# A hybrid attention trunk on one core: four k-tiles of x turned by the DMA crossbar, memory scores in split form, a new warm-up

## The chip, the cores and the metric

The kernel runs on one NeuronCore of a Trainium2 chip. The metric is the device time of one execution in microseconds, here the median of three runs. A profiled execution of the same program gives the span, the engine times and the waits that are read below.

## What is computed

The reference, cut to what matters (one layer, batch 1, 256 tokens, width 2048, all float32):

```python
h = rmsnorm(x, norm_mix_g)                      # x: 256 x 2048
proj = h @ w_in                                 # w_in: 2048 x 8192
dq, dk, dv, mq, mk, mv, gate = split(proj)      # 8 differential heads, 8 block heads, gate slab
lam = exp(sum(lq1 * lk1)) - exp(sum(lq2 * lk2)) + 0.2
d_out = rmsnorm((softmax(q1 k1) - lam * softmax(q2 k2)) @ v, subln_g) * 0.8   # causal, ALiBi
m_out = softmax(q k) @ v                        # causal, ALiBi; with 256 tokens only the own block
x = x + (concat(d_out, m_out) * silu(gate)) @ w_out
q = rmsnorm(x, norm_mem_g) @ w_q_mem            # 4 heads of 128
km, vm = split(rmsnorm(mem, mem_norm_g) @ w_kv_mem)
x = x + (softmax(q km / sqrt(128)) @ vm) @ w_o_mem
out = rmsnorm(x, final_g)
```

## The kernel before

Everything large goes through TensorE as a product of split numbers. A float32 operand a is written as hi + lo, both in the fast 32-bit format (fp32r), and a product is hi·hi + hi·lo + lo·hi, three matmuls into one PSUM bank. The weights stream in as "halves" of 2 k-tiles x 512 columns (0.5 MB). SP issues their loads into 8 raw slots (`w_raw`), ACT makes `w_hi` with a copy (`split_hi`), DVE makes `w_lo` with a subtraction (`split_lo`), PE does 12 matmuls of 512 columns per half (`half_group`). A slot is loaded again once DVE has split what was in it: `load_pair_half` waits for `lo_made` to reach the half's number less 7.

The 16 halves of a window are one pair of heads: halves 0 to 7 give the pair's queries and keys, 8 to 15 its values and gate. Eight windows (4 of differential heads, 4 of block heads) are followed by the tail: the output projection, the memory keys and queries, the memory attention, the last projection.

The first window is special, since x has to be turned first: the contraction runs over x's 2048 columns, so PE needs x with its columns on the partitions, as 16 k-tiles of 128 x 256. In `transpose_rows` (line 637) PE turns k-tile k in two fp32 transposes against the identity into a PSUM bank; ACT writes `aT_hi` with the norm's gain (`rows_out_hi`, line 885) and DVE `aT_lo` (`rows_out_lo`, line 1214). `first_half_group` then does, for every k-tile, 2 matmuls of hi·hi (line 650), 2 of lo·hi (line 654), 2 of hi·lo (line 658), each behind a wait for the piece that it uses. `ROWS_BEHIND` says behind which k-tile which later ones are turned: after k-tile 10 the last four, 12 to 15.

Elsewhere the kernel turns float32 data with the DMA crossbar: ACT or DVE writes the low and high 16-bit halves of each number apart ("planes"), SP issues a DMA transpose of the planes, and DVE or ACT merges them again (`turn_qk`, `turn_y`, `split_turn`, `merge_turn`). SP issues these transposes from the same instruction stream as the weight loads.

What sets the order around the change is written out by hand: the list of instructions of each engine, in which the steps above have their places. SP's queue in the first window holds x in five parts and halves 0 to 17.

In the tail, `transpose_queries` (line 761) turns the memory queries, ACT and DVE copy them out of PSUM, and `memory_scores` (line 772) multiplies them with the memory keys in plain fp32: 8 instructions of 256 columns, which the trace shows as 16 passes. Before the first window PE multiplies the identity with itself (`keep_busy`, line 624) 3 times, later 2 times. Three norm vectors (`gains`, 33 rows) are loaded by ACT's DMA queue and turned on PE behind k-tile 1 (line 629). Lambda is brought to all partitions by a product with a row of ones (line 731).

Of the kernel before, what the change touches and what calls it, by code (L numbers as in the profile page):

```python
# [22 lines left out]
F32 = mybir.dt.float32  # L23
# [78 lines left out]
WARM_UP = (3, 2)  # L102
# [31 lines left out]
def program(nc, x, mem, norm_mix_g, w_in, lambda_q1, lambda_k1, lambda_q2, lambda_k2,  # L134
            subln_g, w_out, norm_mem_g, mem_norm_g, w_q_mem, w_kv_mem, w_o_mem, final_g, out):
    with ExitStack() as ctx:
# [24 lines left out]
        ones_row = sbuf("ones_row", [1, P])  # L161
# [6 lines left out]
        gains = sbuf("gains", [2 * KO + 1, P])  # L168
# [30 lines left out]
        r_rows = y_sb[:, :, 0:P]  # L199
        junk_row, _ = carve(pool, 0, DM)  # L200
# [6 lines left out]
        qmT_sb, at = carve(pool, at, 4, SEQ)  # L207
# [20 lines left out]
        assert at <= NT * DM  # L228
        block_planes, block_planesT = [], []
# [65 lines left out]
        gains_loaded = sem("gains_loaded")  # L295
        warm_ready = sem("warm_ready")
# [22 lines left out]
        km_turned = [sem("km_turned0"), sem("km_turned1")]  # L319
        x_summed = sem("x_summed")  # L320
# [5 lines left out]
        ones_ready = sem("ones_ready")  # L326
        lam_made = sem("lam_made")
# [43 lines left out]
        qmT_ready = sem("qmT_ready")  # L371
# [39 lines left out]

        def qm_rows(g, hf):

            if g == 1:
                return kT_rows[:, 2 * hf:2 * hf + 2], (qT_hi, qT_lo)[hf], 0
            if g == 0:
                return cT_hi, cT_lo, 2 * hf
            return yT_hi, yT_lo, (g - 2) * GK + 2 * hf

        def merged_rows(b):  # L420

            source, n = TURNS[b]
            return mems[:, :, n * COLS:(n + 1) * COLS] if source == "mem" else block_planes[b % 2]

# [21 lines left out]
        def _(sp):  # L446
# [56 lines left out]
            for n in range(PAIR_HALVES):  # L503
# [4 lines left out]
                else:  # L508
                    load_pair_half(DIFF, 0, 0, n)
                if n == 6:  # L510
# [61 lines left out]
        def _(pool_e):  # L572
            pool_e.memset(ident[:, :], 0.0).then_inc(ident_ready, 1)
            pool_e.memset(warm, 0.0).then_inc(warm_ready, 1)
# [14 lines left out]
            pool_e.memset(ones_row[:, :], 1.0).then_inc(ones_ready, 1)  # L589
# [3 lines left out]
        def _(pe):  # L593
# [26 lines left out]
            def keep_busy(count):  # L620


                with pe.Fori(0, count):
                    pe.matmul(ps[:, 2, 0:P], ident[:, :], ident[:, :], start=True, stop=True)  # L624

            def transpose_gains():

                pe.wait_ge(gains_loaded, 48)
                pe.transpose(ps[:, 2, 0:2 * KO + 1], gains[:, :], ident[0:2 * KO + 1, 0:2 * KO + 1]
                             ).then_inc(gainsT_made, 1)  # L630
# [9 lines left out]
            def first_half_group(n):  # L640
# [3 lines left out]
                for i in range(GK // 2):  # L644
# [19 lines left out]
                    if k == 1:  # L664
# [43 lines left out]
            def pair_window(j, kind, first=False):  # L708

                for n in range(PAIR_HALVES):  # L710
# [12 lines left out]
                    if first:  # L723
                        if n == 10:
# [6 lines left out]
                            pe.matmul(ps[:, 6, SEQ:SEQ + 1], ones_row[:, :], neg_lam_row[0:1, :], start=True, stop=True  # L731
# [4 lines left out]

            pe.wait_ge(ident_ready, 2)
            keep_busy(WARM_UP[0])
# [27 lines left out]
            def memory_scores():  # L766

                pe.wait_ge(qmT_ready, 2)
                pe.wait_ge(kmT_ready, 2)
# [99 lines left out]
        def _(act):  # L869
# [12 lines left out]
            def rows_out_hi(k):  # L882

                act.wait_ge(rows_made, k + 1)
# [180 lines left out]
            for row, vec in ((0, norm_mem_g), (KO, mem_norm_g)):  # L1065
                act.dma_start(gains[row:row + KO, :], vec[0].rearrange("(k p) -> k p", p=P)).then_inc(gains_loaded, 16)
            act.dma_start(gains[2 * KO:2 * KO + 1, :], subln_g).then_inc(gains_loaded, 16)
# [45 lines left out]
            for i in range(2 * len(TAIL)):  # L1113
# [26 lines left out]
                if i == 48:  # L1140
# [4 lines left out]
                                   ).then_inc(qm_ready, 1)  # L1145
                if i == 49:
# [464 lines left out]
```

## Time and profile before

| | before |
|---|---|
| median of 3 runs | 573.35 us (573.34 to 574.11) |
| the profiled execution, its own time | 572.92 us |
| its span, first to last instruction | 571.1 us |
| PE busy | 562.1 us (98%) |
| DVE, ACT, POOL busy | 425.9, 406.6, 2.1 us |
| mean granted clock of TensorE | 0.996 |
| moved by DMA | 123.32 MB, mean 216 GB/s |

The chain of work that ended last is followed backwards from the last instruction; here PE makes 98% of it. A wait that is not on that chain costs nothing. PE's times in the chain run from the start of one instruction to the start of the next; a busy time of one matmul (some 390 ns for 512 columns) contains the pipeline's own length and overlaps with its neighbours.

### The profile page before, as it was taken

How to read it: one execution, taken by the hardware profiler on the slowest of the kernel's cores; microseconds unless marked ns; L12 is line 12 of the kernel's file. 1: busy time of each engine (PE TensorE's matmuls, PEld its weight loads, DVE VectorE, ACT ScalarE, POOL GpSimd, SP SyncE). 2: the span in 40 equal slices, each digit the busy share in tenths (PEclk: the TensorE clock that was granted, in tenths of full speed). 3: DMA queues.
4: the chain of work that ended last, by engine and by line, in shares of the span. 5: the costliest groups of instructions: out<-in, count | busy, mean ns of one | idle time of the engine just before them, and what ended most of it. 6: DMA issues, size and time to landing. Idle time of an engine off the chain costs nothing.

```text
span 571.1 us, 8602 instructions
## 1 busy us (share of the span) xinstructions
PE 562.1 (98%) x2640; PEld 468.0 (82%) x2640; DVE 425.9 (75%) x716; ACT 406.6 (71%) x651; POOL 2.1 (0%) x26
## 2 busy tenths in 40 slices
PE   8999999999999999999999999999999999999994
PEld 7888888888888888888888888888888888888884
DVE  4769769678886877866756768668568886877975
ACT  5786866967868778776784784875598786855543
POOL 1000000000000000000000000000000000000000
PEclk9999999999999999999999999999999999999998
DMA  8997769568676776886875976779799986983803
GB/s 272 353 280 238 210 173 250 169 201 230 190 233 192 200 216 188 234 224 163 250 215 157 264 199 192 220 194 299 246 229 266 260 248 187 260 230 111 244 2 147
DMA packets 151236, 123.32 MB, mean 216 GB/s; under 512 B 66809, under 2 KB 133162, under 8 KB 150698
## 3 DMA queue, kind: packets, MB, share of 16 engines
q1 hardware_dynamic: 151112, 122.98, 76.3%
q8 instruction: 12, 0.20, 0.1%
q14 instruction: 14, 0.11, 0.1%
q10 hardware_dynamic: 98, 0.03, 0.0%
HBM read 105.93 MB, written 2.10 MB: 189 GB/s over the span
## 4 chain that ended last, share of the span: by engine, by line
PE 98%; DVE 1%; ACT 0%; POOL 0%; issue 0%; ACTq 0%; POOLq 0%
PE ps L614 28%; PE ps L615 28%; PE ps L616 28%; PE ps L697 2%; PE ps L650 1%; PE ps L654 1%; PE ps L658 1%; PE ps L679 1%; PE ps L850 1%; PE ps L855 1%; PE ps L851 1%; PE ps L637 1%; PE ps L772 1%; PE ps L624 0%; PE ps L818 0%; PE ps L682 0%
## 5 line engine op out<-in xcount | busy, mean ns | idle before, releaser
L1209 DVE TENSOR_TENSOR w_lo<-w_raw,w_hi 128x1024 fp32r<-128x1024 f32 x183 | 222.5, 1222 | 106.2 <-ACT w_hi L880 104.2
L880 ACT ACTIVATE w_hi<-w_raw 128x1024 fp32r<-128x1024 f32 x183 | 192.6, 1057 | 82.3 <-PE ps L616 81.3
L614 PE MATMUL ps<-w_hi,aT 128*128 128x512 f32 x540 | 211.8, 392 | 0.0
L615 PE MATMUL ps<-w_lo,aT 128*128 128x512 f32 x540 | 210.3, 389 | 0.0
L616 PE MATMUL ps<-w_hi,aT 128*128 128x512 f32 x540 | 210.1, 389 | 0.0
L616 PEld LDWEIGHTS ps<-w_hi,aT 128*128 128x128 f32 x540 | 101.4, 188 | 21.2
L614 PEld LDWEIGHTS ps<-w_hi,aT 128*128 128x128 f32 x540 | 101.4, 188 | 21.0
L615 PEld LDWEIGHTS ps<-w_lo,aT 128*128 128x128 f32 x540 | 101.4, 188 | 20.4
L614 PE MATMUL ps<-w_hi,yT_hi 128*128 128x512 f32 x144 | 56.2, 390 | 0.0
L616 PE MATMUL ps<-w_hi,yT_lo 128*128 128x512 f32 x144 | 56.0, 389 | 0.0
L615 PE MATMUL ps<-w_lo,yT_hi 128*128 128x512 f32 x144 | 56.0, 389 | 0.0
L615 PEld LDWEIGHTS ps<-w_lo,yT_hi 128*128 128x128 f32 x144 | 27.0, 188 | 5.6
L614 PEld LDWEIGHTS ps<-w_hi,yT_hi 128*128 128x128 f32 x144 | 27.0, 188 | 5.6
L616 PEld LDWEIGHTS ps<-w_hi,yT_lo 128*128 128x128 f32 x144 | 27.0, 188 | 5.5
L1266 DVE RECIPROCAL pool<-pool 128x128 f32<-128x128 f32 x32 | 30.5, 953 | 1.1
L985 ACT ACTIVATE mems<-ps 128x1024 uint16<-128x1024 uint16 x16 | 15.5, 1021 | 17.0 <-PE ps L616 16.9
L1006 ACT ACTIVATE pool<-pool,small 128x256 f32<-128x256 f32 (+1 forms) x48 | 21.2, 444 | 6.9 <-DVE small L1301 6.9
L955 ACT ACTIVATE pool<-mems 128x1024 uint16<-128x1024 uint16 x16 | 21.8, 1365 | 1.1 <-DMA mems<-mems 1.1
L1293 DVE SCALAR_TENSOR_TENSOR pool<-ps,small,alibi 128x256 f32<-128x256 f32 (+2 forms) x32 | 15.0, 511 | 5.9 <-PE ps L685 5.9
L946 ACT ACTIVATE probT<-mems 128x768 uint16<-128x768 uint16 x16 | 16.0, 1077 | 0.0
L1020 ACT ACTIVATE mems<-pool 128x768 uint16<-128x768 uint16 x16 | 13.3, 832 | 2.9 <-DVE pool L1318 2.9
L885 ACT ACTIVATE aT<-ps,gainsT 128x256 fp32r<-128x256 f32 x16 | 7.5, 470 | 8.8 <-PE ps L637 8.7
(202 smaller groups left out, 569.1 us busy)
## 6 DMA issues: line engine op xcount, KB each, us to landing
w_raw<-in_w_in SPq DMA_DIRECT2D x251, 256.0 KB, 3.2
w_raw<-in_w_out SPq DMA_DIRECT2D x64, 256.0 KB, 4.0
w_raw<-in_w_kv_mem SPq DMA_DIRECT2D x32, 256.0 KB, 4.5
w_raw<-in_w_q_mem SPq DMA_DIRECT2D x16, 256.0 KB, 3.0
w_raw<-in_w_o_mem SPq DMA_DIRECT2D x16, 256.0 KB, 3.8
mems<-in_mem SPq DMA_DIRECT2D x1, 2048.0 KB, 10.1
xs<-in_x SPq DMA_DIRECT2D x3, 512.0 KB, 6.3
w_raw<-in_w_in SPq DMA_DIRECT2D x10, 128.0 KB, 5.5
```

The costliest lines, as they stand in the source:

```text
L614: pe.matmul(acc, hi[:, k0 + k, tok], w_hi[:, slot, k], start=first and k == 0, stop=False)
L615: pe.matmul(acc, hi[:, k0 + k, tok], w_lo[:, slot, k], start=False, stop=False)
L616: m = pe.matmul(acc, lo[:, k0 + k, tok], w_hi[:, slot, k], start=False, stop=last and k == GK // 2 - 1)
L880: act.activation(w_hi[:, i % SPLITS], raw, ACT.Copy).then_inc(hi_made, 1)
L946: act.activation(probT[:, u].rearrange("p i q -> p (i q)").bitcast(U16) .rearrange("p (c h) -> p h c", h=2), probT_planes[:, u].rearrange( ...
L955: act.activation(qkT_sb[:, :, t * P:(t + 1) * P].bitcast(U16) .rearrange("p i (q h) -> p h i q", h=2), qkT_planes[:, t].rearrange("p (h i ...
L985: act.activation(qk_planes[:, t].rearrange("p (h c) -> p h c", h=2), ps[:, t, :].bitcast(U16).rearrange("p (c h) -> p h c", h=2), ACT.Copy ...
L1006: m = act.activation(prob_sb[:, u, c, cols], prob_sb[:, u, c, cols], ACT.Exp, bias=neg_max[:, u, t, c:c + 1], accum_out=exp_sum[:, c, u, t ...
L1020: act.activation(prob_planes[:, u].rearrange("p (h c) -> p h c", h=2), prob_sb[:, u, 0, :].bitcast(U16).rearrange("p (c h) -> p h c", h=2) ...
L1209: dve.tensor_tensor(lo, w_raw[:, i % RAW], hi.bitcast(F32), ALU.subtract).then_inc(lo_made, 1)
L1266: dve.reciprocal(s, s).then_inc(silu_steps, 1)
L1293: dve.scalar_tensor_tensor(prob_sb[:, u, 0:kind.maps, cols], banks[:, :, cols], r[:, t:t + 1], bias, ALU.mult, ALU.add).then_inc(logits_re ...
```

## The change

1. **Crossbar.** k-tiles 12 to 15 of x are no longer turned by PE. POOL writes the 16-bit planes of token tile 0 and ACT those of token tile 1 (128 x 1024 half-words each, from x's last 512 columns). SP issues two DMA transposes behind the loads of half 13 (`X_TURN_BEHIND = 13`). DVE merges both tiles (two copies of 128 x 1024 half-words) between the splits of halves 7 and 8, and ACT and DVE make hi and lo of the four k-tiles from SBUF.
2. **x and its order.** x's fifth part is loaded ahead of half 5, no longer ahead of half 6.
3. **Memory scores.** Queries and keys are split into hi and lo (keys: one ACT copy and one DVE subtraction of 128 x 1024; queries: two of each of 128 x 512, in place of one copy on each engine), and the scores are 24 matmuls of 256 columns in fp32r.
4. **Norm vectors.** `gains` is a full 128 x 128 tile, cleared by POOL; its three loads move from ACT's DMA queue to SP's, behind half 2; PE turns it behind k-tile 6 instead of 1.
5. **Warm-up and lambda.** PE multiplies a tile of ones, made by DVE, 5 times (then 2 times) instead of the identity 3 times; lambda is a product over 128 rows with that tile.

The core of the diff; behind the tables of constants and `rows_split` its pieces belong, in this order, to SP, POOL, ACT, DVE and PE:

```diff
-X_PART_BEFORE = (0, 1, 2, None, 3, None, 4, None)
+X_PART_BEFORE = (0, 1, 2, None, 3, 4, None, None)
+X_TURN_BEHIND = 13
-ROWS_BEHIND = {0: (2,), 1: (3,), 2: (4, 5), 4: (6, 7), 6: (8, 9, 10, 11), 10: (12, 13, 14, 15)}
+ROWS_BEHIND = {0: (2,), 1: (3,), 2: (4, 5), 4: (6, 7), 6: (8, 9, 10, 11)}
-WARM_UP = (3, 2)
+WARM_UP = (5, 2)
...
+        def rows_split(t):
+            return (xq_planes[:, t].bitcast(U16).rearrange("p (h c) -> p h c", h=2),
+                    xs[:, t, 3 * COLS:4 * COLS].bitcast(U16).rearrange("p (c h) -> p h c", h=2))
...
+                if n == 2:
+                    sp.wait_ge(gains_zeroed, 1)
+                    for row, vec in ((0, norm_mem_g), (KO, mem_norm_g)):
+                        sp.dma_start(gains[row:row + KO, :], vec[0].rearrange("(k p) -> k p", p=P)
+                                     ).then_inc(gains_loaded, 16)
+                    sp.dma_start(gains[2 * KO:2 * KO + 1, :], subln_g).then_inc(gains_loaded, 16)
+                if n == X_TURN_BEHIND:
+                    for t in range(NT):
+                        sp.wait_ge(xq_planes_ready[t], 1)
+                        sp.dma_start_transpose(xq_planesT[:, t].bitcast(U16).rearrange("p (i q) -> p i q", q=P),
+                                               xq_planes[:, t].bitcast(U16)).then_inc(xq_turned[t], 16)
...
+            out, rows = rows_split(0)
+            pool_e.wait_ge(x_loaded[4], 16)
+            pool_e.tensor_copy(out, rows).then_inc(xq_planes_ready[0], 1)
...
             rows_out_hi(11)
+            out, rows = rows_split(1)
+            act.wait_ge(x_loaded[4], 16)
+            act.activation(out, rows, ACT.Copy).then_inc(xq_planes_ready[1], 1)
             split_hi(7, 7, 0)
+            sum_squares(0, 0)
+            split_hi(8, 8, 0)
             rows_out_hi(12)
-            sum_squares(0, 0)
             rows_out_hi(13)
-            split_hi(8, 8, 0)
+            sum_squares(1, 0)
             rows_out_hi(14)
-            sum_squares(1, 0)
             rows_out_hi(15)
...
             split_lo(7, 7)
+            for t in range(NT):
+                dve.wait_ge(xq_turned[t], 16)
+                dve.tensor_copy(xq_planes[:, t].bitcast(U16).rearrange("p (k q h) -> p h k q", q=P, h=2),
+                                xq_planesT[:, t].bitcast(U16).rearrange("p (h k q) -> p h k q", h=2, q=P)
+                                ).then_inc(xq_merged, 1)
+            split_lo(8, 8)
             rows_out_lo(12)
             rows_out_lo(13)
-            split_lo(8, 8)
...
-                        m = pe.matmul(ps[:, (4, 0)[t] + h // 2, (h % 2) * SEQ:(h % 2 + 1) * SEQ],
-                                      qmT_sb[:, h, t * P:(t + 1) * P], kmT_sb[:, h, :], start=True, stop=True)
+                        pe.matmul(acc, qmT_hi[:, h, tok], kmT_hi[:, h], start=True, stop=False)
+                        pe.matmul(acc, qmT_hi[:, h, tok], kmT_lo[:, h], start=False, stop=False)
+                        m = pe.matmul(acc, qmT_lo[h // 2][:, h % 2, tok], kmT_hi[:, h], start=False, stop=True)
```

How the change moves instructions is shown at three places. The first is SP's queue in the first window, of the changed kernel, from the lambda vectors on. L482 is the weight load (two of 0.25 MB per half: halves 7, 8, 9 and so on), L545 the new transpose.

```order
L482 DMA w_raw<-in_w_in 128x2x256 x2
L482 DMA w_raw<-in_w_in 128x2x256 [waits lo_made]
L482 DMA w_raw<-in_w_in 128x2x256
...
L482 DMA w_raw<-in_w_in 128x2x256 [waits lo_made]
L482 DMA w_raw<-in_w_in 128x2x256
L545 DMA_TRANSPOSE mems<-mems 128x8x128 [waits xq_planes_ready_pool]
L545 DMA_TRANSPOSE mems<-mems 128x8x128 [waits xq_planes_ready_act]
L482 DMA w_raw<-in_w_in 128x2x256 [waits lo_made]
L482 DMA w_raw<-in_w_in 128x2x256
```

The two rows above the transposes load half 13, those below half 14. In the kernel before, nothing stood between them.

The second place is DVE from the split of half 5 on. Before (L1209 is `split_lo`, L1214 `rows_out_lo`):

```order
L1209 TENSOR_TENSOR w_lo<-w_raw,w_hi 128x1024 [waits hi_made]
L1214 SCALAR_TENSOR_TENSOR aT<-ps,gainsT,aT 128x256 [waits rows_hi]
L1209 TENSOR_TENSOR w_lo<-w_raw,w_hi 128x1024 [waits hi_made]
L1214 SCALAR_TENSOR_TENSOR aT<-ps,gainsT,aT 128x256 [waits rows_hi]
L1209 TENSOR_TENSOR w_lo<-w_raw,w_hi 128x1024 [waits hi_made]
L1214 SCALAR_TENSOR_TENSOR aT<-ps,gainsT,aT 128x256 [waits rows_hi] x2
L1209 TENSOR_TENSOR w_lo<-w_raw,w_hi 128x1024 [waits hi_made]
```

and the same place of the changed kernel (L1262 is `split_lo`, L1273 and L1270 are `rows_out_lo` from PSUM and from SBUF, L1476 the merge):

```order
L1262 TENSOR_TENSOR w_lo<-w_raw,w_hi 128x1024 [waits hi_made]
L1273 SCALAR_TENSOR_TENSOR aT<-ps,gainsT,aT 128x256 [waits rows_hi]
L1262 TENSOR_TENSOR w_lo<-w_raw,w_hi 128x1024 [waits hi_made]
L1273 SCALAR_TENSOR_TENSOR aT<-ps,gainsT,aT 128x256 [waits rows_hi]
L1262 TENSOR_TENSOR w_lo<-w_raw,w_hi 128x1024 [waits hi_made]
L1476 COPY mems<-mems 128x2x512 [waits xq_turned0]
L1476 COPY mems<-mems 128x2x512 [waits xq_turned1]
L1262 TENSOR_TENSOR w_lo<-w_raw,w_hi 128x1024 [waits hi_made]
L1270 SCALAR_TENSOR_TENSOR aT<-mems,gainsT,aT 128x256 [waits rows_hi] x2
```

Two merges that wait for the transposes have come in, and the split of half 8 (the row below them) now stands ahead of the low parts of k-tiles 12 and 13.

The third place is PE behind k-tile 10 (L658 and L699 end a k-tile). Before:

```order
L658 MATMUL ps<-w_lo,aT 128x512
L637 MATMUL ps<-ident,xs 128x128 [waits rows_lo,x_loaded4]
L637 MATMUL ps<-ident,xs 128x128
...
L637 MATMUL ps<-ident,xs 128x128 [waits rows_lo,x_loaded4]
L637 MATMUL ps<-ident,xs 128x128
L650 MATMUL ps<-w_hi,aT 128x512 [waits hi_made,rows_hi]
```

and in the changed kernel:

```order
L699 MATMUL ps<-w_lo,aT 128x512
L691 MATMUL ps<-w_hi,aT 128x512 [waits hi_made,rows_hi]
L691 MATMUL ps<-w_hi,aT 128x512
L695 MATMUL ps<-w_hi,aT 128x512 [waits rows_lo]
L695 MATMUL ps<-w_hi,aT 128x512
```

The eight transposes are gone, and k-tile 11 follows k-tile 10 directly. The row that waits for k-tile 12 comes six matmuls later.

## Rows read from the trace of the kernel before

**Rows 1.** The page: its first line and part 1, PE.
```profile
span 571.1 us, 8602 instructions
PE 562.1 (98%) x2640; PEld 468.0 (82%) x2640; DVE 425.9 (75%) x716; ACT 406.6 (71%) x651; POOL 2.1 (0%) x26
```

**Rows 2.** Waits of PE over the span: waited for, us in total, times, longest.
```profile
PE ps L624 <- POOL ident L578: 1.7, 1, 1.7
```

**Rows 3.** The chain that ended last, 22 to 28 us: start, us, what.
```profile
24.21 0.87 PE ps L637 x8
...
26.46 0.45 PE ps L650 x2
26.91 0.45 PE ps L654 x2
```

**Rows 4.** Timeline of SP: weight loads, then the first DMA transposes of the kernel.
```profile
15.05 9.56 SPq L456 DMA_DIRECT2D w_raw<-in_w_in  x14
34.59 3.87 SPq L475 DMA_TRANSPOSE mems<-mems  x2
```

**Rows 5.** DMA, 0 to 24.66 us and 0 to 34.59 us: all that was moved.
```profile
DMA packets 7163, 7.56 MB, mean 307 GB/s; under 512 B 538, under 2 KB 6394, under 8 KB 7162
...
DMA packets 10765, 11.04 MB, mean 319 GB/s; under 512 B 751, under 2 KB 9996, under 8 KB 10764
```

**Rows 6.** Line L475, then L482, both 128 x 1024 half-words: from issue to landing.
```profile
L475 SPq DMA_TRANSPOSE mems<-mems x16: 1234/1242/2397, 34.6 to 359.2; - x16
DMA to landing us min/median/max: 3.1/3.3/5.3
...
L482 SPq DMA_TRANSPOSE pool<-mems x7: 1231/1232/1571, 92.1 to 368.2; - x7
DMA to landing us min/median/max: 4.7/5.0/6.2
```

**Rows 7.** SP and DMA at 36 us: the second transpose's issue and its landing.
```profile
36.05 2.40 SPq L475 DMA_TRANSPOSE mems<-mems  x1
...
mems<-mems SPq DMA_TRANSPOSE x1, 4.6
```

**Rows 8.** Timeline of ACT and DVE, 22 to 24 us.
```profile
22.13 0.47 ACT L885 ACTIVATE aT<-ps,gainsT 128x256 fp32r<-128x256 f32 x1
...
22.50 1.22 DVE L1209 TENSOR_TENSOR w_lo<-w_raw,w_hi 128x1024 fp32r<-128x1024 f32 x1
```

**Rows 9.** Groups by form: plane copy, merge, low part from SBUF (mean ns).
```profile
L917 ACT ACTIVATE pool<-xs 128x1024 uint16<-128x1024 uint16 x8 | 8.3, 1043 | 0.0
...
L1229 DVE COPY mems<-pool 128x1024 uint16<-128x1024 uint16 x8 | 5.6, 750 | 0.0
L1240 DVE SCALAR_TENSOR_TENSOR aT<-mems,gainsT,aT 128x256 fp32r<-128x256 f32 x16 | 6.7, 477 | 0.0
```

**Rows 10.** The chain at the start: k-tile 0, and the gains' transpose.
```profile
5.62 1.04 PE ps L650 x2
6.66 0.46 PE ps L654 x2
...
9.66 0.18 PE ps L629
```

**Rows 11.** Busy times by stretch: PE, PEld, DVE, ACT, POOL, granted clock, DMA share, GB/s.
```profile
566.20:571.00 4.80, 0.00 (x0) 0.00 (x0) 0.81 (x3) 1.07 (x2) 0.00 (x0) 0.50 0.61 219
```

**Rows 12.** Tail: the chain at the memory scores; timeline of 256-column matmuls and of PE's last.
```profile
518.44 3.45 PE ps L772 x16
...
562.29 0.28 PE L850 MATMUL ps<-w_hi,cT_hi 128*128 128x256 f32 x1
562.41 0.28 PE L851 MATMUL ps<-w_lo,cT_hi 128*128 128x256 f32 x1
...
563.25 0.64 PE L855 MATMUL ps<-w_hi,cT_lo 128*128 128x256 f32 x4
```

**Rows 13.** Timeline of weight loads into PE at the start.
```profile
7.60 0.20 PEld L637 LDWEIGHTS ps<-ident,xs 128*128 128x128 f32 x2 [0.45 <-DMA xs<-in_x]
```

More of the change, by code:

```diff
@@ L167, in program @@
         mix_gain = sbuf("mix_gain", [KO, P])
-        gains = sbuf("gains", [2 * KO + 1, P])
+        gains = sbuf("gains", [P, P])
         gainsT = sbuf("gainsT", [P, 3 * KO + 1])
@@ L199, in program @@
         r_rows = y_sb[:, :, 0:P]
+        ones = r_row[:, 0:P]
         junk_row, _ = carve(pool, 0, DM)
@@ L410, in program @@
         kT_rows = kT_parts[:, :, :, :].rearrange("p u r s -> p (u r) s")
+        qmT_hi = kT_rows
+        qmT_lo = (qT_hi, qT_lo)
+        kmT_hi, kmT_lo = cT_hi, cT_lo
         def qm_rows(g, hf):
@@ L573, in _ @@
             pool_e.memset(ident[:, :], 0.0).then_inc(ident_ready, 1)
+            pool_e.memset(gains[:, :], 0.0).then_inc(gains_zeroed, 1)
             pool_e.memset(warm, 0.0).then_inc(warm_ready, 1)
@@ L623, in keep_busy @@
                 with pe.Fori(0, count):
-                    pe.matmul(ps[:, 2, 0:P], ident[:, :], ident[:, :], start=True, stop=True)
+                    pe.matmul(ps[:, 2, 0:P], ones, ones, start=True, stop=True)
             def transpose_gains():
                 pe.wait_ge(gains_loaded, 48)
-                pe.transpose(ps[:, 2, 0:2 * KO + 1], gains[:, :], ident[0:2 * KO + 1, 0:2 * KO + 1]
-                             ).then_inc(gainsT_made, 1)
+                pe.transpose(ps[:, 2, 0:P], gains[:, :], ident[:, :]).then_inc(gainsT_made, 1)
             def transpose_rows(k):
@@ L730, in pair_window @@
                             pe.wait_ge(lam_ready, 2)
-                            pe.matmul(ps[:, 6, SEQ:SEQ + 1], ones_row[:, :], neg_lam_row[0:1, :], start=True, stop=True
+                            pe.matmul(ps[:, 6, SEQ:SEQ + 1], ones, neg_lam_row[:, :], start=True, stop=True
                                       ).then_inc(lam_made, 1)
@@ L882, in rows_out_hi @@
             def rows_out_hi(k):
+                if k >= 3 * GK:
+                    act.wait_ge(xq_merged, NT)
+                    rows, hi = rows_turned(k, aT_hi)
+                    act.activation(hi, rows, ACT.Identity, scale=gainsT[:, k:k + 1]).then_inc(rows_hi, 1)
+                    return
                 act.wait_ge(rows_made, k + 1)
@@ L1145, in _ @@
                                    ).then_inc(qm_ready, 1)
+                    act.wait_ge(kmT_ready, 2)
+                    act.activation(kmT_hi[:, :, :], kmT_sb[:, :, :], ACT.Copy).then_inc(kmT_hi_ready, 1)
                 if i == 49:
-                    act.wait_ge(qmT_made, 1)
-                    act.activation(qmT_sb[:, 0:2].rearrange("p h s -> p (h s)"), ps[:, 4, :], ACT.Copy
-                                   ).then_inc(qmT_ready, 1)
+                    for b in range(2):
+                        act.wait_ge(qmT_made, b + 1)
+                        act.activation(qmT_hi[:, 2 * b:2 * b + 2], ps[:, 4 + b, :].rearrange("p (h s) -> p h s", s=SEQ),
+                                       ACT.Copy).then_inc(qmT_hi_ready, 1)
                 if i == 41:
@@ L1401, in row_rms @@
                 rsqrt(r, ms, newton[:, 0:NT], steps, extra + 1)
+            dve.memset(ones, 1.0).then_inc(ones_ready, 1)
+            dve.memset(neg_lam_row, 0.0).then_inc(lam_zeroed, 1)
             dve.wait_ge(gainsT_made, 1)
```

50 lines of the change are left out of this document (37 added, 13 removed).

## The prediction

> **What bounds the kernel now.** I read the page first, then PE's waits, the chain, and last SP and the DMA in the first 35 us. PE is busy for 98% of the span [rows 1], and its only wait for another engine is one of 1.7 us at the start [rows 2]; beside it stands a gap of 0.45 us at 7.60 for the second part of x [rows 13]. So every microsecond that PE is spared comes off the time, and every microsecond that it waits is added: nothing later takes a wait back. SP and the DMA don't appear there, because the weights come early enough. How early, and over what queue, decides this change: from 15.05 to 24.61 SP issues 14 weight loads, halves 7 to 13 [rows 4], and at 24.66 only 7.56 MB have been moved [rows 5].
>
> **What PE is spared.** The eight transposes of k-tiles 12 to 15 take 0.87 us [rows 3]. The gains' transpose goes from behind k-tile 1, 0.18 us [rows 10], to behind k-tile 6, where a transpose of 128 columns costs 0.87/8 = 0.11: 0.07 less. The memory scores take 3.45 us now; the new ones are 24 matmuls of 256 columns, which follow each other at 562.41 - 562.29 = 0.12 us [rows 12], so 2.88 and 0.57 less. Together 1.5 us, if nothing else happened: 573.35 - 1.5 = 571.8.
>
> **Edits that I cost at nothing.** The longer warm-up and its tile of ones come before 7.60, where PE waits 0.45 us for x anyway [rows 13]. An earlier rise of the clock would only lengthen that wait. If the ten passes ran late they have the same 0.45 us; beyond that it is a loss of some tenths. The lambda product keeps its passes. The gains' loads put three more issues into SP's queue, 0.5 us each at most by the weight loads beside them; the queue of data behind SP is then megabytes long, so the DMA has work meanwhile. The extra splits of the scores' operands (one ACT copy of about 1 us [rows 9], one DVE subtraction of 1.22 us [rows 8], and four short ones) stand beside matmuls of the half in between, 12 times 0.23 us [rows 10]; they cost something only if the queries' low parts come later than 2.7 us after their transpose, and then DVE is what PE waits for.
>
> **The crossbar path, step by step.** PE now needs k-tile 12 at 26.46 - 0.87 - 0.07 = 25.5 [rows 3]. When does it get it?
>
> 1. *Planes.* ACT copies token tile 1 after `rows_out_hi(11)`, which ends at 22.60 [rows 8]; the copy takes 1.04 us [rows 9], so 23.65. POOL has no such copy in this trace. It starts once x's last part is there, and has until the queue below is empty; it costs nothing up to several microseconds, and I take nothing.
> 2. *Issue.* SP reaches the transposes behind half 13's loads, at about 24.6 [rows 4].
> 3. *The queue.* All these transfers are of SP's queue. By 24.6 it holds x (2.10 MB) and 14 halves (14 x 0.524 = 7.34 MB), 9.44 MB, of which 7.56 are moved [rows 5]. The other 1.88 MB are ahead of the transposes. From 24.66 to 34.59 the DMA moves 11.04 - 7.56 = 3.48 MB, 0.35 MB per us, so they need 5.4 us: until 30.0. That transposes do wait behind loads shows in two lines with the same shape: those of L475, issued mostly with little ahead, land 3.3 us after issue, those of L482, issued among weight loads, 5.0 [rows 6].
> 4. *Landing of both.* The nearest case is the pair at 34.59 [rows 4]. By then 2.10 + 18 x 0.524 = 11.53 MB had been issued and 11.04 moved; the last 0.49 MB went by 36.0. The second landed 4.6 us after 36.05, at 40.65 [rows 7]: 4.65 us behind an empty queue. The other end: its issue long done, the pair needs the 3.3 us of a lone one [rows 6]. Behind 30.0 this gives 33.3 to 34.65. I take 34.0, in the middle, since SP can issue the first of the two early but is itself held back by the full queue.
> 5. *Merge.* The second merge takes 0.75 us [rows 9]: 34.75. ACT's high part (0.47 us) lets PE start the first pair of k-tile 12 at about 35.2.
> 6. *Low part.* DVE first splits half 8, 1.22 us [rows 8], then makes the low part of k-tile 12, 0.48 us [rows 9]; overlapped as they usually are 1.65 us together: 36.4. Only then can the third matmul of k-tile 12 run. In the kernel before it ran at 26.91 [rows 3].
>
> So that matmul is 36.4 - 26.9 = 9.5 us later than before, the savings ahead of it included. Behind it DVE is ahead of PE again (low parts of 0.48 us against 1.38 us of matmuls per k-tile), and the buffers are full.
>
> **The clock.** PE stands still from 25.5 to 35.2. At the end of the kernel the clock stands at 1.2 GHz (0.50) from 566.20 on [rows 11], less than 3 us after PE's last matmuls began at 563.25 [rows 12]; so it falls in this gap. At the start PE worked from 1.7 on [rows 2] and the rate doubled around 6.4: two matmuls of 512 columns took 1.04 us at 5.62 and 0.46 at 6.66 [rows 10]. With the same 4.7 us of slow clock from 35.2 on, the part behind 36.4, 3.5 us, does half its work: 1.75 us lost. The bounds are nothing and some 3 us. The Trainium skill has this too (TensorE: Matmul & The Clock Gate, section "HAM oscillation — how this bites in real kernels"): a wait for DMA brings the slow clock back, in its case with 1.67 us at the slow clock per gap, half of it lost; by that figure the loss would be 0.8 and the time 583.1. This trace shows the longer phase at its start, and I go by it.
>
> **The sum.** +9.5 (stall, with PE's savings before it) + 1.75 (clock) - 0.57 (scores) = +10.7. The profiled execution took 572.92 us, 0.43 less than the median, so 583.6 against itself and **584.0** against the median of 573.35.
>
> A second page bears on step 4 (the Trainium skill, DMA: Bandwidth & Descriptors, section "Latency and other measured facts"): a DMA transpose moves 261 GB/s. An estimate by it: 0.52 MB take 2.0 us behind 30.0, and the sum is 582.0. The pair in this trace took 4.65 us, which decides against it.
>
> **Rivals.**
>
> - *A. The clock stays up, or falls only briefly.* The stall is as above, the 1.75 us are not lost: 582.2. For it: nothing in this trace shows a gap of PE in the middle. Against it: the drop at the end [rows 11].
> - *B. The transposes don't queue behind the loads.* Then the second is issued at 24.6 + 1.24 and lands 3.3 us later [rows 6], at 29.1; merge, split and low part end at 31.5; the third matmul is 4.6 us late, the clock costs 1.75 more: 573.35 + 4.6 + 1.75 - 0.57 = 579.1. Against it: L482's 5.0 us, and that step 3 counts 1.88 MB ahead of them.
> - *C. Not slower: the turned rows are there when PE comes.* Its place is the gap ahead of k-tile 12, its price the 1.5 us of PE work alone: 571.8, faster by 0.27%. It decides if both transposes have landed by about 23.8, for merge, high part and low part to be ready at 25.5 to 26. SP would have to reach them by 20. For it: SP's pace is set by the full queue, which x's earlier fifth part reorders. Against it: the load of half 13 waits for the split of half 5, and ACT's planes exist only at 23.65. Even an empty queue gives B. The break-even is a stall of 1.5 us.
> - *D. Longer.* SP can't issue the transposes before the queue has nearly drained, or the slow clock holds longer than at the start: 34.65 in step 4 and up to 3 us for the clock give 586.
>
> **How the numbers follow.** The forecast gets 0.66, A 0.14, B 0.10, D 0.06, C 0.04. What is told apart from no change is 0.2%, 1.1 us. Slower by more: forecast, A, B and D, 0.96. Faster by more: nearly all of C, 0.03. Within: 0.01. The range takes the forecast with step 4's ends and the clock's bounds (33.3 and no loss give 581.5; 34.65 and 3 us give 586), and goes down to B: **578.5 to 586.5**.
>
> **What would show it.** In the changed kernel's profile: PE's waits gain one, of 9 to 10 us, ahead of k-tile 12, released by ACT's high part, and a shorter one for DVE's low part behind it. DVE waits some 8 us for the transpose ahead of its merges (L1476). The transposes (L545) take 8 us and more to land. The granted clock of the stretch 30 to 40 us is below 1. The chain loses the eight transposes, and the scores (L816 to L818) take 2.9 us. The prediction is wrong if the transposes land within 4 us of their issue (B), if PE's wait is under 2 us (C), if the scores cost more than 3.45 us because PE waits there for DVE, or if a stall of this size stands and the time is nevertheless under 580, which would mean that PE's work is not what sets the end.

## The result, and the profile after

The changed kernel takes **583.72 us** (median of 4 executions, 583.35 to 584.15) against 573.35: a ratio of 1.0178, 95% interval 1.0163 to 1.0192, slower by 10.4 us. The forecast was 584.0, range 578.5 to 586.5. The execution that was profiled took 584.15; its span is 582.3, 11.2 more than in [rows 1], and the mean granted clock of TensorE is 0.984 (before 0.996). Two executions far outside the rest, one of the kernel before (2025.54 us) and one of a later experiment (1468.61 us), are in none of the medians, ratios and intervals below.

First the page of the kernel after, the lines that answer to [rows 1], and the granted clock in tenths over 40 slices of the span:

```profile
span 582.3 us, 8623 instructions
...
PE 564.2 (97%) x2644; PEld 469.6 (81%) x2644; DVE 429.5 (74%) x722; ACT 409.7 (70%) x654; POOL 3.1 (1%) x27
...
PEclk9959999999999999999999999999999999999998
```

PE is busy 2.1 us longer than before, though it has less to do, and the third slice (29 to 44 us) stands at 5 tenths. So the 11.2 us are a stall, and slower work behind it. The wait of PE, then those of ACT and DVE on the same chain (us in total, times, longest):

```profile
PE ps L691 <- ACT aT L932: 9.5, 1, 9.5
...
ACT aT L932 <- DVE mems L1476: 7.5, 1, 7.5
DVE mems L1476 <- DMA mems<-mems: 6.9, 2, 6.7
```

(PE's only other wait is one of 1.1 us at the start, for DVE's tile of ones, where the kernel before waits 1.7 [rows 2].) Read from top to bottom these are one event: PE waits for the high part of k-tile 12, ACT for the merge, DVE for the DMA transpose. The timelines of SP and DVE (start, us, engine and operation, in brackets the idle time before it and what ended it):

```profile
16.34 9.63 SPq L482 DMA_DIRECT2D w_raw<-in_w_in  x14
26.01 5.95 SPq L545 DMA_TRANSPOSE mems<-mems  x2
...
33.05 0.74 DVE L1476 COPY mems<-mems 128x1024 uint16<-128x1024 uint16 x1 [6.69 <-DMA mems<-mems]
33.97 0.74 DVE L1476 COPY mems<-mems 128x1024 uint16<-128x1024 uint16 x1 [0.18 <-DMA mems<-mems]
34.60 1.21 DVE L1262 TENSOR_TENSOR w_lo<-w_raw,w_hi 128x1024 fp32r<-128x1024 f32 x1
```

And the line of the transposes (duration of an issue in ns, least, median and most; first and last start), with its time from issue to landing:

```profile
L545 SPq DMA_TRANSPOSE mems<-mems x2: 2350/2950/3549, 26.0 to 29.6; - x2
...
DMA to landing us min/median/max: 4.3/5.7/7.0
```

SP reaches the pair at 26.01, is held in it for 5.95 us, and the second lands at 33.95, 2.0 us after its issue has ended. The chain that ended last, from there to the first matmul of half 8:

```profile
29.61 4.33 DMA mems<-mems
...
33.97 0.75 DVE mems L1476
34.74 0.52 ACT aT L932
...
35.30 1.22 PE ps L691 x2
36.52 0.95 PE ps L695 x2
37.48 0.85 PE ps L699 x2
...
40.89 0.68 PE ps L691 x2
41.57 0.47 PE ps L695 x2
...
43.88 0.23 PE ps L656
```

L695 at 36.52 is the third matmul of k-tile 12, which ran at 26.91 [rows 3]: **9.61 us** later. The 0.85 us per two matmuls behind it are the slow clock (0.45 to 0.47 once it is over, at 41.57). Half 8 begins at 43.88, in the kernel before at 31.97:

```profile
31.97 0.23 PE ps L614
```

That is 11.91 us later, so in this execution the slow clock cost 11.91 - 9.61 = **2.30 us**. The granted clock by stretch (column behind POOL's busy time; then DMA share and GB/s):

```profile
24.50:27.00 2.50, 1.27 (x5) 0.68 (x4) 1.24 (x2) 2.47 (x4) 0.00 (x0) 1.00 1.11 349
27.00:30.00 3.00, 0.00 (x0) 0.00 (x0) 0.00 (x0) 0.22 (x1) 0.00 (x0) 0.60 1.10 346
...
35.30:41.20 5.90, 5.90 (x14) 4.38 (x15) 3.67 (x8) 3.45 (x7) 0.00 (x0) 0.50 0.57 186
41.20:43.90 2.70, 2.70 (x13) 2.21 (x12) 1.23 (x1) 2.67 (x4) 0.00 (x0) 0.99 0.52 178
```

From here on the two kernels run alike, and the lag shrinks twice. At the lambda product it goes from 11.91 to 11.63 (L772 here, L731 in the kernel before). At the memory scores (chain, 24 matmuls from 530.14 to 533.01, one each 0.12 us) it goes from 11.70 to 11.12, with no wait for DVE or ACT. The kernel before at the lambda product, then the kernel after at both places:

```profile
40.36 0.31 PE ps L731 x2
40.67 0.43 PE ps L614
```

```profile
52.27 0.12 PE ps L772 x2
52.38 0.34 PE ps L656
...
530.14 0.12 PE ps L816
530.25 0.12 PE ps L817
```

The books of the span: +9.61 + 2.30 - 0.28 (lambda product) - 0.58 (scores) = +11.05, and the spans differ by 11.2.

### The profile page after: what moved, and what is told of

Read it like the earlier page. It is cut to its first block, busy times and chain, and to the rows that moved or that the text cites. A ratio compares the mean times of both kernels' runs of the same rounds, so it can differ in the third digit from the quotient of the medians.

```text
span 582.3 us, 8623 instructions
## 1 busy us (share of the span) xinstructions
PE 564.2 (97%) x2644; PEld 469.6 (81%) x2644; DVE 429.5 (74%) x722; ACT 409.7 (70%) x654; POOL 3.1 (1%) x27
## 4 chain that ended last, share of the span: by engine, by line
PE 94%; SPq 2%; DMA 1%; DVE 1%; ACT 1%; issue 0%; ACTq 0%
PE ps L656 27%; PE ps L657 27%; PE ps L658 27%; PE ps L738 2%; SPq L482 1%; PE ps L720 1%; PE ps L895 1%; PE ps L900 1%; PE ps L896 1%; PE ps L691 1%; PE ps L695 1%; PE ps L699 1%; DMA mems<-mems 1%; DMA w_raw<-in_w_in 1%; SPq L545 1%; PE ps L863 0%
## 5 line engine op out<-in xcount | busy, mean ns | idle before, releaser
L1262 DVE TENSOR_TENSOR w_lo<-w_raw,w_hi 128x1024 fp32r<-128x1024 f32 x183 | 222.7, 1222 | 107.8 <-ACT w_hi L925 105.8
L656 PE MATMUL ps<-w_hi,aT 128*128 128x512 f32 x540 | 211.7, 392 | 0.0
L658 PE MATMUL ps<-w_hi,aT 128*128 128x512 f32 x540 | 210.2, 389 | 0.0
L658 PEld LDWEIGHTS ps<-w_hi,aT 128*128 128x128 f32 x540 | 101.4, 188 | 21.2
L656 PEld LDWEIGHTS ps<-w_hi,aT 128*128 128x128 f32 x540 | 101.4, 188 | 21.0
L658 PE MATMUL ps<-w_hi,yT_lo 128*128 128x512 f32 x144 | 56.0, 389 | 0.0
L658 PEld LDWEIGHTS ps<-w_hi,yT_lo 128*128 128x128 f32 x144 | 27.0, 188 | 5.6
L691 PE MATMUL ps<-w_hi,aT 128*128 128x512 f32 x32 | 12.2, 469 | 9.7 <-ACT aT L932 9.5
L691 PEld LDWEIGHTS ps<-w_hi,aT 128*128 128x128 f32 x32 | 6.5, 222 | 11.4 <-ACT aT L932 10.0
```

Of the source, the lines that this page charges most:

```text
L656: pe.matmul(acc, hi[:, k0 + k, tok], w_hi[:, slot, k], start=first and k == 0, stop=False)
L658: m = pe.matmul(acc, lo[:, k0 + k, tok], w_hi[:, slot, k], start=False, stop=last and k == GK // 2 - 1)
L691: pe.matmul(ps[:, t, :], aT_hi[:, k, t * P:(t + 1) * P], w_hi[:, slot, i], start=first, stop=False)
L1262: dve.tensor_tensor(lo, w_raw[:, i % RAW], hi.bitcast(F32), ALU.subtract).then_inc(lo_made, 1)
```

## The experiments

All are edits of the kernel after, unless said otherwise; the ratio is always to the kernel before on the same chip (medians there 573.35 to 573.77).

**Does the place in SP's list set the stall?** The edit is one constant, earlier by two halves, or later (15):

```diff
-X_TURN_BEHIND = 13
+X_TURN_BEHIND = 11
```

> The changed kernel with the transposes two halves earlier in SP's queue (behind half 11, not 13). Theory (the pair waits for all bytes that stand ahead of it): 1.05 MB less ahead, at 0.35 MB per us 3.0 us; the pair lands at 31 in place of 34, PE's wait ahead of k-tile 12 falls from 10.0 to 7 us, the time to 580.7 us. Rival (the pair takes as long as it takes once planes exist, 24.1 us, since the crossbar is slow under load): landing stays near 34, the time 583.7. Second rival (SP's place doesn't matter because ACT's planes come late): under 1 us gained.

> The changed kernel with the transposes two halves later (behind half 15). Theory: 1.05 MB more ahead, 3.0 us later, PE's wait 13 us, 586.7 us. Rival (the pair's landing is set by its planes and the crossbar): 583.7.

Measured: 580.48 us, ratio 1.0120 (1.0099 to 1.0141), and 586.01 us, 1.0220 (1.0199 to 1.0241). PE's wait is 6.5 and 12.3 us. SP's timeline and DVE's second merge, behind half 11:

```profile
23.82 6.03 SPq L545 DMA_TRANSPOSE mems<-mems  x2
...
31.88 0.74 DVE L1476 COPY mems<-mems 128x1024 uint16<-128x1024 uint16 x1 [0.16 <-DMA mems<-mems]
```

and behind half 15:

```profile
28.59 6.04 SPq L545 DMA_TRANSPOSE mems<-mems  x2
...
36.69 0.74 DVE L1476 COPY mems<-mems 128x1024 uint16<-128x1024 uint16 x1 [0.17 <-DMA mems<-mems]
```

The three kernels have one picture, shifted: the pair's issue takes 6.0 us, and the second merge comes 2.0 to 2.1 us behind its end (29.85, 31.96, 34.63 against 31.88, 33.97, 36.69). Each place of two halves is worth 2.1 to 2.7 us of the merge, where the theory had 3.0, and 2.3 to 3.2 of the time (it had 580.7 and 586.7). The landing follows the number of loads ahead.

A rival that the two edits can't tell apart from this is a fixed delay of some 4 us between SP's arrival and the first packet. The packets under 512 B show it in slices of 0.2 us (a transpose's have 0.25 KB): they set in at 28.0, 29.8 and 32.8, that is 4.2, 3.8 and 4.2 us after SP's arrival, with 1.6, 1.5 and 1.6 MB of x and weights issued and not yet moved. The pair of [rows 4] had only 0.49 MB ahead, and its packets set in at 35.8, 1.2 us after 34.59. So the delay goes with the bytes ahead, and a fixed one is ruled out. It is the same 4 us in the three kernels because SP itself runs about 1.6 MB ahead of the DMA in each.

**Does it wait behind SP's queue, or behind the DMA's work?** Here ACT issues the two transposes, in its own queue; they stand in its list behind its plane copy, and each waits only for its planes:

```diff
-                if n == X_TURN_BEHIND:
-                    for t in range(NT):
-                        sp.wait_ge(xq_planes_ready[t], 1)
-                        sp.dma_start_transpose(xq_planesT[:, t].bitcast(U16).rearrange("p (i q) -> p i q", q=P),
-                                               xq_planes[:, t].bitcast(U16)).then_inc(xq_turned[t], 16)
...
+            for t in range(NT):
+                act.wait_ge(xq_planes_ready[t], 1)
+                act.dma_start_transpose(xq_planesT[:, t].bitcast(U16).rearrange("p (i q) -> p i q", q=P),
+                                        xq_planes[:, t].bitcast(U16)).then_inc(xq_turned[t], 16)
```

> The changed kernel with both transposes issued by ACT, right behind its plane copy (24.1 us), so in a DMA queue of their own; SP's queue holds loads only. Theory (waiting behind the loads in the same queue is what makes them late): they land 3.3 to 5 us after issue, at about 28 and 30; merges done by 31; PE's wait is 6 us, the time about 579 to 580. Rival (the DMA engines are full, whatever the queue): the pair lands near 34, 583.7 us; it may even be later, since ACT's split of half 7 moves behind two issues.

Measured: 584.29 us, ratio 1.0196 (1.0176 to 1.0215). Not faster: my theory of "behind the loads of the same queue" fell in this form. Its timelines of ACT's queue and of DVE:

```profile
21.82 1.41 ACTq L1134 DMA_TRANSPOSE mems<-mems  x1
...
24.20 2.95 ACTq L1134 DMA_TRANSPOSE mems<-mems  x1
...
30.84 0.74 DVE L1475 COPY mems<-mems 128x1024 uint16<-128x1024 uint16 x1 [1.27 <-DMA mems<-mems]
34.54 0.74 DVE L1475 COPY mems<-mems 128x1024 uint16<-128x1024 uint16 x1 [2.96 <-DMA mems<-mems]
```

And its DMA queues in 25 to 26, in 25 to 28 and in 28 to 30 us (packets, MB, share of 16 engines; in 25 to 26 there is no row but the one shown):

```profile
q1 hardware_dynamic: 359, 0.35, 110.0%
...
q10 hardware_dynamic: 502, 0.13, 24.5%
...
q1 hardware_dynamic: 569, 0.55, 80.7%
q10 hardware_dynamic: 569, 0.14, 32.3%
```

ACT's first is issued 4.2 us earlier than SP's was (it waits for POOL's planes alone and goes out before ACT's own plane copy has run), yet the second lands at 34.5. q10 is ACT's queue. It moves nothing before 26.0, 4.2 us after its first transpose was issued, though POOL's planes had been ready since 20.2 and nothing else stood in that queue. At 21.82 SP had issued x and the loads up to half 10 (7.86 MB, and one or two loads more), of which 6.38 MB were moved; those 1.5 MB take 4.2 us at 0.35 MB per us. So a queue of its own didn't pass the backlog: the pair waited as long as in SP's queue. Why it waits for loads of the other queue no run shows; that the time fits their bytes is an estimate. Behind 26.0, while both queues have work, the DMA engines take one packet of each in turn (569 and 569): a load's packet has about 1 KB, a transpose's 0.25, so each small packet pays for a large one. The 2112 packets of the two transposes take until 34.5. What the pair waits for is the full DMA, by either queue. The Trainium skill has the sharing (DMA: Bandwidth & Descriptors, section "Issuing engines are not separate DMA queues"): transfers interleave on the same 16 engines whoever issues them. The trace agrees, with its 569 packets of each queue.

**What did the clock cost?** PE fills its gap with products of ones, into a bank that nobody reads, so that it doesn't stand still (`GAP` is 40, then 25):

```diff
+                    if k == 3 * GK:
+                        with pe.Fori(0, GAP):
+                            pe.matmul(ps[:, 3, P:2 * P], ones, ones, start=True, stop=True)
```

> The changed kernel with 40 products of the tile of ones put ahead of k-tile 12, into a PSUM region that nobody reads (some 8.5 us at the fast clock), so that PE waits as long for x but is not idle. Theory (2.3 us of the 10.4 lost are the slow clock behind the wait): granted clock 1.00 from 35 us on, k-tiles 12 to 15 take 1.38 us each again, the time 581.4 us. Rival (those k-tiles are slow for want of operands, not of clock): no change, 583.7. If the loop outlasts the wait, its excess is added.

Measured: 586.87 us, ratio 1.0235 (1.0218 to 1.0252). The loop was longer than the gap: 40 products took 15.07 us, and the third matmul comes at 41.21 in the chain, 4.7 later than in the kernel after. The clock did stay up: two matmuls take 0.46 us from there on. By the sum +4.7 - 2.3 the profiled execution would be 2.4 slower; the spans (584.7 and 582.3) differ by 2.4. With 25 products:

> As gap_busy with 25 products instead of 40. There 40 of them took 14.9 us, 5.4 longer than PE's wait, though the clock stayed at 1.00 behind them and k-tiles 12 to 15 took 1.37 us each. 25 should take 9.3 us, as long as the wait. Theory (the slow clock behind the wait costs 2.3 us): 581.4 us. Rival (the filling itself slows DVE, ACT or the transposes by what it saves): 583.7.

Measured: 582.36 us, ratio 1.0155 (1.0139 to 1.0172); the intervals of this and of the kernel after overlap, the medians differ by 1.4. The trace shows it directly. Its busy times by stretch (columns as above):

```profile
35.00:42.00 7.00, 6.11 (x27) 4.60 (x27) 5.76 (x10) 6.31 (x11) 0.00 (x0) 1.00 0.67 200
```

And its chain from the third matmul of k-tile 12 on, with the last two of half 7:

```profile
36.82 0.73 PE ps L699 x2
37.55 0.46 PE ps L703 x2
...
41.64 0.45 PE ps L703 x2
```

The granted clock is 1.00 at once, and the stretch from the third matmul (L699 here) to half 8 takes 42.10 - 36.82 = 5.28 us, where the kernel after needs 43.88 - 36.52 = 7.36 and the kernel before 5.06. Against the profiled execution of the kernel after, the slow clock is worth 2.1 to 2.3 us. The idle gap is its cause: filling the gap with useless work takes it away.

Its size is another matter. The other kernels with a gap ahead of k-tile 12 have the same matmuls behind it, so the same subtraction can be done in each (starts in the chain; the slow phase runs from PE's first matmul behind the gap to the rise of the granted clock; the loss is the time from the third matmul to half 8, less the 5.06 us of the kernel before):

| kernel | PE's wait | slow phase | third matmul | half 8 | lost |
|---|---|---|---|---|---|
| kernel after | 9.5 | 5.9 | 36.52 | 43.88 | 2.30 |
| pair in ACT's queue | 10.1 | 4.8 | 37.10 | 43.90 | 1.74 |
| pair behind half 15 | 12.3 | 3.9 | 39.24 | 45.60 | 1.30 |
| low parts first (below) | 8.6 | 3.9 | 35.52 | 41.87 | 1.29 |
| pair behind half 11 | 6.5 | 3.7 | 34.44 | 40.74 | 1.24 |
| early pair (below) | 4.2 | 4.7 | 31.53 | 38.40 | 1.81 |

In all six the granted clock is 0.50 behind the gap, and the length of the slow phase doesn't go with the length of the gap. So 2.30 is the largest of six readings, from one execution each, and 1.2 to 1.8 is what the others show. The 1.4 us between the medians of the kernel after and of the kernel with 25 products is nearer to those.

**Is the low part behind half 8's split worth anything?** DVE makes the low parts of k-tiles 12 and 13 first:

```diff
-            split_lo(8, 8)
...
             rows_out_lo(13)
+            split_lo(8, 8)
```

> The changed kernel with DVE making the low parts of k-tiles 12 and 13 ahead of the split of half 8. Theory: k-tile 12's low part is ready 0.9 us earlier, but PE's first pair of that k-tile takes 0.85 us at the slow clock, so its third matmul moves from 36.52 to about 36.15: 0.4 us less, 583.3 us. Rival (the split of half 8 is what comes late then): no change.

Measured: 583.72 us, ratio 1.0170 (1.0156 to 1.0184). In its trace the low part is ready in time, but the first two matmuls behind the gap take 1.22 us anyway (the expectation had 0.85), and the third comes at 35.52 behind a start at 34.30: the same 1.22 as from 35.30 to 36.52 in the kernel after. That all of it comes 1.0 us earlier is not the edit: SP reached the pair at 24.93 in this execution, which is also the fastest of the five (582.13; the others 583.53 to 583.89). The time is not told apart from the kernel after. The trace speaks for no gain; the intervals don't exclude one of up to half a microsecond.

**What is the rest of the change worth, without the crossbar?** PE turns k-tiles 12 to 15 again and x's order is that of before; the warm-up, the gains' tile, the lambda product and the scores stay as changed. A second kernel puts the old scores back as well. A third is the kernel before with only the new scores.

> The changed kernel with the crossbar part and the order of x undone (k-tiles 12 to 15 turned by PE again), the rest of the change kept. Theory (the whole loss is the crossbar's wait and what follows it; the rest is PE work taken away): scores -0.57, lambda product -0.28 (read from the changed kernel's chain), gains -0.07: 0.9 us below the kernel before, 572.4 us, ratio 0.9984. Rival (the start costs a few tenths: gains in SP's queue, longer warm-up): 572.8 to 573.3.

> As no_crossbar, with the memory scores in plain fp32 again, so the kernel before with the new gains, warm-up and lambda product alone. Theory: -0.28 -0.07, 573.0 us, ratio 0.9994. Rival (the start costs): 573.3 to 573.7.

> The kernel before with the split memory scores alone. Theory: 24 passes at 0.12 us for 3.45 us, -0.57: 572.8 us, ratio 0.9990. Rival (the wait for the queries' low parts takes it back): 573.3, with a wait of PE on DVE at the scores.

Measured: 572.32 us, ratio 0.9982 (0.9972 to 0.9991, 11 executions); 573.04 us, 0.9997 (0.9988 to 1.0006); 573.17 us, 0.9997 (0.9988 to 1.0006). So everything but the crossbar gives 0.2%, and the crossbar with its order of x costs 583.72 - 572.32 = 11.4 us (11.2 by the two ratios, since the runs were on different chips). The first two say that the scores bring 0.7 us, with 0.57 expected. The third agrees only in its trace (2.87 us for the scores, 3.45 in [rows 12]); its interval reaches from 0.7 us faster to 0.3 slower, which holds both 0.57 and nothing, so its time decides nothing. Of lambda product, gains and warm-up together nothing measurable is left in the second kernel. The first is the fastest kernel of the study.

**Can the crossbar pay at all?** If the stall is the arrival, an earlier pair must shorten it. x's last part goes ahead of half 3, ACT's planes behind k-tile 5, the transposes behind half 6:

```diff
-X_PART_BEFORE = (0, 1, 2, None, 3, 4, None, None)
-X_TURN_BEHIND = 13
+X_PART_BEFORE = (0, 1, 2, 4, 3, None, None, None)
+X_TURN_BEHIND = 6
```

> The changed kernel with x's fifth part loaded ahead of half 3, ACT's plane copy behind k-tile 5 and the transposes behind half 6, so that they stand behind 5.8 MB, not 9.4. Theory: that much has moved by 20 us, the pair lands at about 24, merges are done when PE asks for k-tile 12 at 25.5: no wait of PE there, and the 0.87 us of PE's transposes are gained as well: 571.5 us, ratio 0.9968. Rival (the pair holds the queue for 3 to 4 us and halves 7 and 8 come late, or SP waits for ACT's planes and the loads behind it stand): new waits of PE at k-tiles 14 and 15, 573 to 577 us.

Measured: 578.66 us, ratio 1.0092 (1.0078 to 1.0106), above the theory's 571.5 and the rival's 573 to 577 alike. PE's wait ahead of k-tile 12 is still 4.2 us. The timelines of SP and ACT:

```profile
15.59 5.72 SPq L545 DMA_TRANSPOSE mems<-mems  x2
...
26.09 1.06 ACT L925 ACTIVATE w_hi<-w_raw 128x1024 fp32r<-128x1024 f32 x1 [3.11 <-DMA w_raw<-in_w_in]
...
29.73 0.90 ACT L932 ACTIVATE aT<-mems,gainsT 128x256 fp32r<-128x256 f32 x2
```

And the DMA's GB/s from 17 to 25 us, in slices of 0.2 us:

```profile
GB/s 359 333 348 338 374 389 379 384 389 374 374 369 348 357 337 298 252 166 96 22 18 106 288 273 293 289 291 288 131 1 0 0 1 26 143 174 251 364 374 384
```

The pair has landed by 23.3, before PE needs it, and ACT comes to it only at 29.73. ACT's list has the splits of halves 7 and 8 and a sum of squares ahead of it, and half 7's weights are late: SP stood in the transposes from 15.59 to 21.31, then issued the four small lambda vectors, and its next weight load starts at 22.72. So the DMA ran dry, at 21 us (18 and 22 GB/s) and again at 23 us (0 and 1). The landing was put right, and the stall moved to the weights.

Two kernels then let ACT and DVE make the turned rows before they split half 7: first k-tiles 12 and 13, then all four (ACT's list of the second; DVE's is changed alike):

```diff
+            for k in range(12, 16):
+                rows_out_hi(k)
...
-            rows_out_hi(12)
-            rows_out_hi(13)
...
-            rows_out_hi(14)
-            rows_out_hi(15)
```

> As early, with the merges ahead of DVE's split of half 6 and the high and low parts of k-tiles 12 and 13 ahead of half 7's split on ACT and DVE. In early the second transpose had landed at 23.3, but ACT made the high part only at 29.7, behind the split of half 7, whose weights came 3.1 us late. Theory (what was left of PE's wait there, 4.2 us, is that order): the merges end at 24.7, PE waits under 1 us at k-tile 12 and another 0 to 1 us at k-tile 14 for half 7, no slow clock: 572 to 573 us, ratio 0.997 to 0.999. Rival (late weights set it): PE's wait moves to k-tile 14 and stays 2 us or more: 574.5 to 576.

> As early_rows_first, with k-tiles 14 and 15 made ahead of the splits of halves 7 and 8 too, on ACT and DVE, and both sums of squares behind them. In early_rows_first PE still waited 1.8 us for the high and 1.25 us for the low part of k-tile 14, both by that order, and 1.1 us at the first scores, whose own transposes stood behind late weights (issued at 37.2, landed 4.5 to 7.1 us later). Theory A (only the order was left): the 3 us go, 1.1 stay: 572.9 us, ratio 0.998. Theory B (the pair has taken 3 to 4 us of the full DMA, and what follows in the queue is late by that): PE comes to the first scores earlier and waits there 3 to 4 us: 574.5 to 576, hardly better. Neither gets below the version without the crossbar (572.3).

Measured: 575.67 us, ratio 1.0031 (1.0018 to 1.0043), and 575.1 us, 1.0030 (1.0020 to 1.0041). The waits of PE in the second:

```profile
PE ps L720 <- DVE kT_parts L1339: 1.2, 1, 1.2
...
PE ps L691 <- ACT w_hi L947: 0.9, 2, 0.6
PE ps L772 <- DVE small L1514: 0.8, 1, 0.8
```

k-tiles 12 to 15 now run without a gap, 0.45 us per two matmuls. But PE waits 2.9 us in all, in four other places. Two are ahead of the turned rows: 0.3 us for k-tile 0's weights at 5.73, which its sister kernel doesn't have, and 0.6 us at 16.49 for a high part of weights, which ACT made behind its plane copy (now behind k-tile 5, where it had waited 1.4 us for x's last part). Two are behind them: 0.8 us for the lambda row and 1.2 for the first scores, whose own transposes SP reached at 37.35, against 34.59 in [rows 4]. Compared with the kernel without the crossbar that is 2.8 us more (575.1 - 572.3), though PE is spared 0.87 us of transposes; 0.8 of it I can't name. The rivals that foresaw 574.5 to 576 for both had the time right, the mechanism only in part: I had put the lag in one wait of 2 us or more, and it came as four. Whether a further reordering of ACT and DVE would win was not tried.

## Why the prediction was right

- **What bounds the kernel** (PE, no slack later): held. A lag of 9.6 us at k-tile 12 was still 10.4 us, with the clock's loss and the savings behind it, at the end, over 530 us later; nothing took it back. Every experiment repeats it.
- **The edits costed at nothing:** the reason given for the warm-up was misread. The 0.45 us at 7.60 are a gap of the weight loads [rows 13]; PE's own timeline of the kernel before has no gap there. The longer warm-up does show at first (the first matmul of k-tile 0 starts at 5.92, in the kernel before at 5.62), and with the gains' transpose moved it is gone by k-tile 4 (11.75 against 11.88). So nothing was the right price, for another reason.
- **Step 1, planes:** ACT's copy runs at 23.10, 1.05 us, as put. POOL's, which the trace before didn't show, takes 1.04 us at 18.50 and hides.
- **Step 2, issue:** forecast 24.6, measured 26.01. The gains' three loads (7.22 to 8.47 in SP's queue) delay all that follow; I had named them and given them nothing.
- **Step 3, the queue:** forecast 30.0. That 1.4 us of delay didn't count, because the queue behind SP still held loads. At 26.01 still 9.44 - 7.93 = 1.51 MB were ahead (7.46 MB moved by 24.66, then 348 GB/s), 4.3 us, until 30.3. The answers on the DMA of the kernel after for 29 to 30, 30 to 31, 31 to 32 and 32 to 33 us show the transposes as packets under 512 B:

```profile
DMA packets 385, 0.34 MB, mean 344 GB/s; under 512 B 58, under 2 KB 385, under 8 KB 385
...
DMA packets 530, 0.24 MB, mean 242 GB/s; under 512 B 386, under 2 KB 530, under 8 KB 530
...
DMA packets 169, 0.05 MB, mean 54 GB/s; under 512 B 155, under 2 KB 169, under 8 KB 169
...
DMA packets 1151, 0.29 MB, mean 287 GB/s; under 512 B 1151, under 2 KB 1151, under 8 KB 1151
```

  They set in at 29.8, as counted. Rival B (no queueing) is refuted by this and by both moved kernels. But "of SP's queue" was too narrow: in ACT's queue the first packets wait 4.2 us as well, and the pair lands no earlier.
- **Step 4, landing:** forecast 34.0, measured 33.95. The middle between two far rows was lucky in its precision. The rows above show what it is made of: the first packets at 30, a hole from 31 to 32 while SP still issues the second, then 1151 packets in one microsecond. I had weighed 261 GB/s, the figure of the Trainium skill (DMA: Bandwidth & Descriptors, section "Latency and other measured facts") for a transpose with a non-contiguous middle dimension, against the 4.65 us of a pair and dropped it. Once the packets flow alone they move 287 GB/s, so the rule is near for the rate; the pair's time is longer by the issue and the hole.
- **Steps 5 and 6:** forecast 34.75, 35.2 and 36.4; measured 34.74, 35.30 and 36.52. PE's own slow first pair (1.22 us) hides most of the low part's lateness.
- **The clock:** forecast +1.75, bounds 0 and 3, measured +2.30 in the profiled execution and +1.24 to +1.81 in five other kernels. The mechanism held, and the size is right only on average: I took the 4.7 us of the start for the slow phase, and it lasted 5.9 here (35.3 to 41.2) and 3.7 to 4.8 in the others. The 4.7 us rest on the pace of the matmuls alone; the column of the granted clock stands at 1.00 there (0 to 8 us of the kernel before). Rival A (the clock stays up) is refuted.
- **PE's savings:** transposes and gains are within the 9.61. Scores 0.57 forecast, 0.58 measured. "The lambda product keeps its passes" missed 0.28 us. In the trace before, the product with one row takes 0.31 us and its successor 0.43, in place of 0.12 and 0.34.
- **The sum:** +9.5 + 1.75 - 0.57 = +10.7 forecast, +11.2 measured in the span and +10.4 between the medians. The profiled execution of before lay 0.43 below its median, that of after 0.43 above. That the forecast of 584.0 stands only 0.3 us from the median is luck: the clock's loss was put 0.55 too low, and against it stand the 0.28 of the lambda product and the 0.86 by which the two profiled executions lie away from their medians.
- **Rival C** (not slower) asked that SP reach the pair by 20. The early kernel did that and landed it at 23.3. It was slower even so, since ACT and the weights were then late: C's condition was not sufficient.
- **The signs:** PE's wait (9.5, said 9 to 10), the shorter one of its weight load for DVE's low part (0.5), the granted clock (0.50) and the scores (2.87, said 2.9) came as written. DVE waited 6.9 us for the pair (said some 8). The transposes took 7.0 and 4.3 us from issue to landing, not "8 us and more": that sign failed, and 4.3 is close to the 4 us that were to speak for B. I had counted from SP's arrival at the pair (26.01 to 33.95 is 7.9 us), the profile counts each from its own issue, and the second's began only at 29.61.

## What to carry to other kernels

On a kernel in which one engine is busy for 98%, price a removed instruction by its own time and a new producer by its arrival: count the bytes ahead of a transfer when it is issued (in this case those of every queue), divide by the rate of the full DMA, and compare with when the consumer stands there. Giving such a transfer another queue, or moving it forward, doesn't make DMA time: the first waited for the same backlog and was then paid in turns with the loads, the second in late weights and late splits. Of a bundle of edits measure the parts: here four gave 0.2% together, and the fifth took 2% away.

## What the runs showed of the hardware

- A pair of DMA transposes (128 x 1024 half-words each) among weight loads holds SP for 5.7 to 6.0 us in all four places tried (6.2 and 6.9 in the two kernels whose PE fills the gap), against 3.87 in [rows 4], and has landed about 2 us later. During that time SP issues nothing else, and the DMA runs down to 17, 18, 36 and 51 GB/s (the lowest slice of 0.2 us in each of the four).
- The pair's first packets move 3.8 to 4.2 us after SP's arrival with 1.5 to 1.6 MB of loads ahead, and 1.2 us after it with 0.49 MB ahead.
- Two queues with work take turns packet by packet, not byte by byte: 569 of 1 KB and 569 of 0.25 KB in 2 us. ACT's queue got a fifth of the bytes.
- In ACT's queue no packet of the first transpose, issued at 21.82, moved before 26.0, though nothing else stood in that queue; SP's queue then had about 1.5 MB ahead.
- The granted clock fell to 0.50 in gaps of 4.2 to 12.3 us, and stayed there for 3.7 to 5.9 us of steady matmuls afterwards (six traces), without growing with the gap; with products of ones in the gap it was 1.00 at the first matmul of k-tile 12.
